# Block-by-block norm and router sums, a per-token root, and a first expert entered on its own count, in a one-core hybrid layer

## What is computed

```python
h = _rmsnorm(xp, norm2_g[l]) * (1 + sc2) + sh2
xp = xp + g2 * _moe(h, lp)
...
logits = (t @ lp['w_router'] + lp['b_router']).astype(jnp.float32)
top_val, top_idx = lax.top_k(logits, TOP_K)
gate = jax.nn.softmax(top_val, axis=-1).astype(x.dtype)
...
hgu = xb @ w_gu[e] + b_gu[e]
...
act = (h_lin + 1) * (h_glu * jax.nn.sigmoid(SWIGLU_ALPHA * h_glu))
return act @ w_down[e] + b_down[e]
```

## Time and profile before

| what | before |
|---|---|
| median of 3 runs | 1333.12 us (1329.91 to 1335.13) |
| profiled execution, its own time | 1331.8 us |
| its span, first to last instruction | 1329.8 us |
| mean granted TensorE clock | 0.944 |
| read from memory | 473.65 MB |

### The profile page before, as it was taken

One profiled execution on the slowest core, in us unless ns is written; L12 is line 12 of the kernel. 1 busy time (PEld: TensorE's weight loads), 2 busy tenths in 40 slices (PEclk: granted clock), 3 DMA queues, 4 the chain that ended last, 5 costly groups with the idle time before them and its releaser, 6 DMA issues.

```text
span 1329.8 us, 25320 instructions
## 1 busy us (share of the span) xinstructions
PE 1126.3 (85%) x10266; PEld 584.0 (44%) x10267; DVE 307.5 (23%) x889; ACT 247.8 (19%) x530; POOL 6.3 (0%) x24
## 2 busy tenths in 40 slices
PE   6999999999999977986897797876696688888795
PEld 4777887788874322332333232322232222333231
DVE  2298234421341211110111111101111111111112
ACT  2321135311031210211111011111110011111112
POOL 1000000000000000000000000000000000000000
PEclk9999999999989988998999899988899899999998
DMA  9998331343467999999999999999999999999996
GB/s 398 423 395 340 127 127 64 119 154 127 156 251 297 396 427 428 401 429 429 429 415 429 429 429 428 429 429 428 428 430 427 429 429 427 428 430 427 429 429 278
DMA packets 35486, 476.21 MB, mean 358 GB/s; under 512 B 3901, under 2 KB 5309, under 8 KB 6623
## 3 DMA queue, kind: packets, MB, share of 16 engines
q1 hardware_dynamic: 33904, 473.92, 85.2%
q10 hardware_dynamic: 1550, 1.84, 0.4%
HBM read 473.65 MB, written 2.10 MB: 358 GB/s over the span
## 4 chain that ended last, share of the span: by engine, by line
PE 49%; DMA 41%; DVE 5%; ACT 2%; issue 2%; DVEq 1%; ACTq 0%; SPq 0%
DMA big<-in_w_down 25%; DMA big<-in_w_gu 15%; PE bank L1613 14%; PE low L1137 10%; PE bank L1645 6%; PE low L1350 3%; PE low L1151 2%; PE bank L1137 2%; DVE big L805 2%; PE bank L1566 2%; PE bank L1530 2%; ACT h L431 2%; PE bank L1619 1%; PE bank L1196 1%; PE bank L1536 1%
## 5 line engine op out<-in xcount | busy, mean ns | idle before, releaser
L1613 PE MATMUL bank<-big,h 128*32 128x512 f32 x2816 | 369.0, 652 | 99.5 <-DMA big<-in_w_gu 95.3
L1613 PEld LDWEIGHTS bank<-big,h 128*32 128x32 f32 x2816 | 82.9, 114 | 324.4 <-issue 177.8
L1645 PE MATMUL bank<-big,h 128*32 128x256 f32 x2816 | 173.4, 396 | 59.2 <-DMA big<-in_w_down 50.2
L1137 PE MATMUL low<-h,big 128*128 128x256 f32 x832 | 187.6, 383 | 0.0
L1137 PEld LDWEIGHTS low<-h,big 128*128 128x128 f32 x832 | 157.1, 191 | 25.2 <-issue 3.2
L431 ACT ACTIVATE side<-bank 128x256 f32<-128x256 f32 (+1 forms) x94 | 36.7, 392 | 614.5 <-PE bank L1530 612.8
L1645 PEld LDWEIGHTS bank<-big,h 128*32 128x32 f32 x2816 | 90.2, 113 | 130.7 <-DMA big<-in_w_down 54.9
L431 ACT ACT_TABLE_LOAD x68 | 87.2, 1283 | 21.3 <-DVE work L947 15.4
L1083 DVE TENSOR_SCALAR h<-bank 128x256 f32<-128x256 f32 x44 | 18.7, 425 | 306.2 <-PE bank L1613 306.2
L1094 DVE TENSOR_TENSOR side<-bank,big 128x512 f32<-128x512 f32 x44 | 30.4, 692 | 202.9 <-PE bank L1645 202.9
L1021 DVE TENSOR_SCALAR side<-iota,work 128x32 f32 (+1 forms) x90 | 17.5, 239 | 212.3 <-issue 212.2
(11 more groups left out here) (258 smaller groups left out, 689.7 us busy)
## 6 DMA issues: line engine op xcount, KB each, us to landing
big<-in_w_gu SPq DMA_DIRECT2D x128, 2048.0 KB, 22.3
big<-in_w_down SPq DMA_DIRECT2D x64, 2048.0 KB, 27.6
big<-in_trunk_w SPq DMA_DIRECT2D x32, 2048.0 KB, 12.9
x<-in_x_t SPq DMA_DIRECT2D x1, 1024.0 KB, 4.8
out_y_tok<-x SPq DMA_DIRECT2D x4, 256.0 KB, 2.5
cinit<-in_c_init_t SPq DMA_DIRECT2D x1, 516.0 KB, 30.3
abias<-in_rpb SPq DMA_DIRECT2D x1, 512.0 KB, 32.3
out_c_new<-abias ACTq DMA_DIRECT2D x1, 512.0 KB
```

What stands on the lines that cost most here:

```text
L1137: ins = pe.matmul(to, w[:, k, b * P:(b + 1) * P], src[:, k, :], start=k == 0, stop=k == KD - 1)
L1613: ins = pe.matmul(up_sum(q), mo["xg"][:, k % 2, k // 2, :], up_weights(expert_slot(e, j), i, q), start=False, stop=k == KD - 1, skip_group ...
L1645: ins = pe.matmul(bank[7][q * SLOTS:(q + 1) * SLOTS, 0:QW], mo["actt"][:, k % 2, k // 2, :], down_weights(expert_slot(e, GU_CHUNKS + j), i ...
```

## The change

1. Block by block: each output block is reported, added to x, squared and scaled by the gain alone (x2g, in h) as it comes. The sums of squares and the raw logits of blocks 0 to 3 are put on PE's queue ahead of block 6, those of 4 to 6 after block 7, those of 7 last. Squares go to four 32-row parts.
2. Per-token root: the four parts of the sum are brought together with tokens on partitions, so that the root is a [128, 2] array; it scales the logits (with the bias, spread over partitions earlier) and the rows of h_tok, in the copy that ACT makes anyway. Scaling, gain and shift of h by block are gone.
3. The shift is not in h_tok any more. It is spread for both conditions (PE, 16 matmuls), and in each pass DVE makes the right one for each slot (shift_slots, two instructions) and adds it to the gathered rows (gath_keep, which was a copy on ACT).
4. The number of passes of expert 0 is kept by itself (first_tab). SP and PE enter expert 0 on it, before the table is made; the table's sums, gate weights and g2 come before or beside the first pass.
5. The residual is added to the output banks after the experts 1 to 3, not before expert 0; ACT clears the banks first (four instructions).

```diff
-            for t in range(4):
-                act.wait_ge(S["mixed"], t + 1)
-                square(t)
-            norm_root(2)
...
+            for k in range(KD):
+                act.wait_ge(S["mixed"], k + 1)
+                func(sq[:, k, :], x[:, k, :], ACT.Square).then_inc(S["squared"], 1)
                 for s in range(2):
...
+                    ins = func(h[:, k, s * L:(s + 1) * L], x[:, k, s * L:(s + 1) * L], ACT.Copy,
+                               scale=gain[:, 1, k, s:s + 1])
+                ins.then_inc(S["x2g_made"], 1)
+            act.wait_ge(S["var"], 2)
+            func(rt["rs"], rt["rs"], ACT.Sqrt).then_inc(S["root"], 1)
+            act.wait_ge(S["shift_made"], 2)
+            func(mo["shift1"], bank[6][:, QW:2 * QW], ACT.Copy).then_inc(S["shift_kept"], 1)
...
+                    func(mo["h_tok"][:, s, half * 512:(half + 1) * 512], turn_h_bank(half, s)[:, :], ACT.Copy,
+                         scale=rt["rs"][:, s:s + 1]).then_inc(S["h2_kept"], 1)
...
+            for b in range(4):
+                func(bank[b][:, :], ones[:, 0:1].to_broadcast([P, 512]), ACT.Copy, scale=0.0
+                     ).then_inc(S["low_cleared"], 1)
...
+            def shift_slots(n, e, base):
+
+                dve.tensor_scalar(rt["ind"], rt["cnt0"][:, bass.ds(e, 1)], iota[:, bass.ds(base, 1)], rt["slotno"],
+                                  ALU.subtract, ALU.is_ge).then_inc(S["shift_step"], 1)
+                dve.wait_ge(S["shift_step"], n * 2 + 1)
+                dve.scalar_tensor_tensor(mo["slot_shift"], mo["shift_gap"], rt["ind"], mo["shift1"],
+                                         ALU.mult, ALU.add).then_inc(S["shift_step"], 1)
+
+            def gath_keep(n):
+
+                dve.wait_ge(S["shift_step"], n * 2 + 2)
+                dve.wait_ge(S["gathered"], n + 1)
+                dve.tensor_tensor(mo["gath"], bank[4][:, 0:QW], mo["slot_shift"], ALU.add).then_inc(S["gath_kept"], 1)
...
-                select(e_next, table(dve, n + 1 + T_BASE, 0, TOK - SLOTS))
+                base = table(dve, n + 1 + T_BASE, 0, TOK - SLOTS)
+                select(e_next, base)
+                shift_slots(n + 1, e_next, base)
+                gath_keep(n + 1)
...
+                    if 4 * c + b == 6:
+                        square_sums(range(4))
+                        raw_sums(range(4))
+                    if c:
+                        pe.wait_ge(S["mixed"], b + 1)
+                    ins = product(C_OUT + c, b, merged, out_block(4 * c + b))
+                    ins.then_inc(S["out_made"] if b < 3 else S["chunk_used"], 1)
+
+            raw_sums(range(4, 7))
+            square_sums(range(4, 7))
+            spread(bank[6], 24, 0).then_inc(S["shift_made"], 1)
+            raw_sums([7]).then_inc(S["raw_logits"], 1)
+            square_sums([7]).then_inc(S["ssq_split"], 1)
+            spread(bank[6], 24, 1).then_inc(S["shift_made"], 1)
             pe.wait_ge(S["lt_ready"], 1)
...
+            pe.wait_ge(S["h2_kept"], 4)
+            gather(0)
             pe.wait_ge(S["np_made"], 1)
...
+            first_passes = pe.value_load(first_tab[0:1, 0:1], min_val=1, max_val=MAX_PASS)
...
+            up_bias()
+            pe.wait_ge(S["gath_kept"], 1)
+            turn2(4, QW, mo["gath"], "xg_turned")
             pe.wait_ge(S["past_made"], 1)
...
-            keep_residual(9, 16)
...
-            pe.wait_ge(S["table_made"], 1)
-            n_pass = table(pe, T_ALL, NE, MAX_PASS)
...
+            with pe.Fori(0, first_passes) as n:
+                expert_pass(n, 0, 0)
+            pe.wait_ge(S["table_made"], 1)
...
+            for e in range(1, TURN):
+                later_passes(0, e)
+            keep_residual()
+            with pe.Fori(1, NE // TURN) as turn:
```

More of the change, by code:

```diff
@@ L359, in _, with later_expert @@
                 load_expert(1, 1, j)
+            sp.wait_ge(S["np_made"], 1)
+            first_passes = sp.value_load(first_tab[0:1, 0:1], min_val=1, max_val=MAX_PASS)
+            for j in range(AHEAD, PER_EXPERT):
+                sp.wait_ge(S["chunk_used"], first_passes * PER_EXPERT + (N_TRUNK + j - AHEAD + 1 - PER_EXPERT))
+                load_expert(1, 1, j)
             sp.wait_ge(S["table_made"], 1)
[L364 to L368, removed]
+            def later_expert(e, i):
+                passes = {early: table(sp, e + (T_BEFORE - early), 1, MAX_PASS) for early in (True, False)}
+                for j in range(PER_EXPERT):
                     used = j - AHEAD + 1 - PER_EXPERT * (j >= AHEAD)
@@ L988, in _ @@
+            dve.wait_ge(S["rs_made"], 1)
+            for s in range(2):
+                ins = dve.scalar_tensor_tensor(rt["lg"][:, s, :], bank[7][:, s * NE:(s + 1) * NE], rt["rs"][:, s:s + 1],
+                                               rt["brsb"][:, s, :], ALU.mult, ALU.add)
+            link(ins)
             for s in range(2):
@@ L1482, in _ @@
-            ins.then_inc(S["raw_logits"], 1)
-            def keep_residual(lo, hi):
-                for u in range(lo, hi):
-                    k, s = u // 2, u % 2
-                    pe.matmul(by_token[:, k // 2, s, (k % 2) * P:(k % 2 + 1) * P], x[:, k, s * L:(s + 1) * L],
-                              ident[:, :], start=u % 4 == 0, stop=False, skip_group_check=True)
-            keep_residual(0, 5)
+                    if 4 * c + b == 6:
+                        square_sums(range(4))
+                        raw_sums(range(4))
@@ L1511, in _ @@
-            turn_h(0, 0)
-            turn_h(0, 1)
+                pe.matmul(bank[7][:, s * NE:(s + 1) * NE], rt["lt"][:, s * L:(s + 1) * L], stack[:, :],
+                          start=True, stop=True)
+            pe.wait_ge(S["ssq_parted"], 2)
+            for s in range(2):
+                ins = pe.matmul(bank[7][:, 400 + s:401 + s], rt["sp"][:, s * L:(s + 1) * L], ones[:, 0:1],
+                                start=True, stop=True)
+            ins.then_inc(S["ssq"], 1)
+            for half in range(2):
+                for s in range(2):
+                    for k in range(4 * half, 4 * half + 4):
+                        pe.wait_ge(S["x2g_made"], k + 1)
+                        ins = pe.transpose(turn_h_bank(half, s)[:, (k % 4) * P:(k % 4 + 1) * P],
+                                           h[:, k, s * L:(s + 1) * L], ident[:, :])
+                    ins.then_inc(S["h2_turned"], 1)
@@ L1519, in _, with keep_residual @@
                 ins = pe.matmul(bank[7][0:NE, 128:129], rt["picked"][:, s, :], ones[:, 0:1], start=s == 0, stop=s == 1)
-            ins.then_inc(S["ranked"], 1)
-            turn_h(1, 0)
-            pe.wait_ge(S["h2_kept"], 1)
-            turn_h(1, 1)
+            pe.matmul(bank[7][:, 360:360 + NE], ones[:, :], rt["picked"][:, 0, :], start=True, stop=True
+                      ).then_inc(S["ranked"], 1)
+            pe.wait_ge(S["shift_kept"], 2)
+            for s in range(2):
+                ins = spread(bank[6], 40, s)
+            ins.then_inc(S["g2_made"], 1)
+            def keep_residual():
+                for k in range(KD):
+                    for s in range(2):
+                        pe.matmul(by_token[:, k // 2, s, (k % 2) * P:(k % 2 + 1) * P], x[:, k, s * L:(s + 1) * L],
+                                  ident[:, :], start=False, stop=False, skip_group_check=True)
             def gather(n):
```

186 lines of the change are left out of this document (88 added, 98 removed).

## The result

| what | before | after |
|---|---|---|
| median of 16 runs each, same chip | 1334.31 us (1328.5 to 1338.24) | 1324.6 us (1322.35 to 1330.0) |
| ratio | | 0.9933 [0.9919, 0.9946] |
| profiled execution, its own time | 1331.8 us | 1323.38 us |
| its span | 1329.8 us | 1321.6 us |
| output product ends (P) | 377.31 | 378.75 |

The kernel is 0.67% faster; 1325 was forecast. P is where the chain leaves the output product, E where the second pass's first up matmul starts. E comes 12.6 us earlier, the end only 8.2. Both numbers need an explanation, the second more.

A forecast was written before the change was run, and what follows sets the result against it. The expert stage lasts as long as its weights stream in, so the stream's start, set by PE's path, moves the end. First matmul -9.7, first pass +2.4, sum -7.3 from 1331.8: 1324.5, stated as 1325 us, range 1318.5 to 1331.5.

The forecast's parts named there:

- inserts and bias, to P: Output product: sums put between its blocks, +1.3 us, and the bias spread ahead of it, +0.3.
- P to logits: From the output product's end to the logits: 9.0 us before, 4.9 now, -4.1.
- logits to positions: Logits to expert ranks: sixteen turns, started earlier, take 4.0 us, ranks and a count about 2; -0.3.
- positions to F: Ranks to first expert matmul: later turns, residual and table wait leave the path; 14.3 us to 7.4, -6.9.
- F: The first expert matmul, claimed to come 9.7 us earlier, at about 395.7.
- first pass: First expert pass, 16.08 us before, would begin at 1.2 GHz with the residual gone from ahead of it: +2.4.
- The early fall: Rival: clock falls during scattered sums behind the product, sixteen turns take 8 us instead of 4; 1329 us, chance 0.25.
- the clock stays up: Rival: full clock for spread, gather, bias and turn saves about 3 us, selection costs 1.0; 1319 us, chance 0.14.
- If the passes behind it keep their length: Condition for the end to move by as much as the first pass's end: later passes last as before.
- The moved residual: Its 16 turns between experts 3 and 4 cost nothing beside PE's weight waits; uncovered, 4 to 8 us.
- The change doesn't reach the end: Rival: the first release comes earlier, but a later wait (ring, residual) gives it back; 1332 us, chance 0.08.
- DVE's lateness: Rival: DVE's longer turn per pass comes after PE's need; 1341 us at 1.4 us late, chance 0.06.

The follow-up runs named there:

- e11: The changed kernel itself, nothing edited, profiled one more time; 1324.62 us in one run.
- e2: Changed kernel, but PE and SP enter expert 0 only after the whole table is made; 1330.15 us, ratio 0.9969 against the kernel before.
- e5: Kernel before, with only its residual moved after expert 3 and the banks cleared by ACT; 1335.36 us, ratio 1.0017 against the kernel before.
- e7: Changed kernel with two extra DVE instructions in each pass, about 0.6 us a pass; 1325.63 us, ratio 0.9934 against the kernel before.
- e10: The changed kernel itself, nothing edited, profiled one more time; 1327.38 us in one run.

## Why the prediction was right

| step | predicted | measured |
|---|---|---|
| inserts and bias, to P | +1.6 | +1.4 |
| P to logits | -4.1 | 9.0 to 4.6: -4.4 |
| logits to positions | -0.3 | 4.8 to 3.7: -1.1 |
| positions to F | -6.9 | 14.3 to 4.4: -9.8 |
| F | -9.7 | -13.9 |
| first pass | +2.4 | 16.08 to 17.35: +1.3 |
| E | -7.3 | -12.6 |
| E to the end | 0 | +4.4 |
| the end | -7.3 | -8.2 |

- **The two structural steps held.** The inserts on the chain, 0.57 and 0.48, are 1.05 against 1.3; the end without any overlap, 3.5, was far off. The logits and the root gave -4.4 against -4.1.
- **The turns were read at twice their price.** "1.97 for four at half" are eight turns, for each is one record; 0.25 a turn is the price at half the clock, not at the full one. The sixteen took 1.95 (382.16 to 384.11), not 4.0. DVE's top four, 2.2 as before, then set this stretch and not PE's turns, and positions came 0.8 sooner than worked out. The early fall's price, 8 for 4, was doubled in the same way.
- **The step that failed is the clock, in both directions.** "I let the pass begin at 1.2 GHz" did not come true in this execution, nor did the half-clock prices of spread, gather and bias, 1.78, 1.93 and 1.93, which were 1.08, 1.07 and 1.06. What came is the rival "the clock stays up", with the 1.0 of selection wait that it named (1.10), and its E of -12.7 (-12.6). Its time of 1319 did not come. The 0.50 wait for the up bias's transfer stood in no term. In e11 the path was part of the way to the forecast, and E - P was 2.8 longer, so of the 14.0 that E - P gained in the first profile some 2.8 belong to the clock of that execution. In e2 and e5 the pass began at 1.2 GHz. The Trainium skill, "TensorE: Matmul & The Clock Gate", Part 1, has the low clock as the default that activity releases, and says that the number of slow matmuls at a kernel's start varies between runs of one kernel. The trace shows such a difference in the middle of a kernel (391.46 and 394.50 for F); the first rule doesn't tell the execution.
- **"If the passes behind it keep their length" failed too.** PE's passes do keep it: the second and third take 16.05, as before. The stream behind them doesn't: its stops, 8.2 against 3.6, gave back 4.4 in this pair of profiles, by luck not far from what the low clock had been charged, 2.9 ahead of the pass and 2.4 in it. The total was right with two errors of opposite sign. The Trainium skill, "TensorE: Matmul & The Clock Gate", section "HAM oscillation", tells of a loop in which the matmuls start slow after each wait for a transfer. Here 32 of the 87 chunks that PE waited for did, and of the nine slow ones on the chain six cost the end nothing.
- **The moved residual** stands between experts 3 and 4 and cost nothing that can be seen, as predicted: the stream has no stop there.

```profile
482.69 3.84 PE L1579 MATMUL low<-ident,x 128*128 128x128 f32 x32
```

Moving it gained nothing either when moved alone (e5). That parts 4 and 5 cover each other was not in the working, which booked the residual, the table's wait and the loads as separate gains.
- **The other rivals.** The clock's early fall, during the sums and turns, came in no profile of the changed kernel; in e11 it fell at 386, behind the turns, and the time was 1324.62. "The change doesn't reach the end" is half true: it came through later stops of the stream and neither at the third pass, where the pause is no longer than before, nor at the residual. DVE's lateness is out (e7).

## What to carry to other kernels

Compare the stretch that the change touches (here E - P) and the whole separately, over several profiles of the same program: single profiles of one kernel differed by 3 us in this stretch and by 6 behind it, over half of what the change is worth. Where two removed steps ran side by side, undo them together as well as singly: each alone looked worth 0.5 and 4.8 us, both together nothing that the interval can tell. Work taken from in front of a weight-bound stage is passed on to the end only as far as the stream behind it stops no longer than before; measure the stops from the landings, for slow chunks on PE's chain alone don't tell them.

## What was not expected of the hardware

- One program's granted clock in one stretch was 1.00 in one execution and 0.50 in another (e10, e11), with nothing but the execution changed.
- An up chunk's eight matmuls take 1.92 at the full clock and up to 3.64 at the low one, a down chunk's sixteen 1.93 and up to 3.64, and waiting for a transfer led to a slow chunk in about a third of the cases: the chunk at 522.21 of the earlier trace rows took 1.93 after a wait of 1.61, and in the changed kernel, the wait being 2.96, the one at 509.29 took 3.48.
- One and the same chunk, issued at the same time in two executions of one program, landed 7.8 and 10.2 us later (547.9 in the first profile, 547.8 in e10).
- Raw sums issued two by two in a column group cost no more than in four groups side by side: sixteen records added 0.48 to the chain, where 32 took 1.08 before. Which of them overlap is not shown.
- A turn (a transpose on PE) leaves one record and takes 0.13 us at the full clock (eight in 1.07), where a residual matmul of the same size leaves two and takes 0.24 (sixteen in 3.84).
